# Two heads on both halves of TensorE's array in a first mixer, and its gate units in quarters

## The chip, the cores and the metric

The kernel runs on one core of a Trainium2 chip. A core has a matrix engine (TensorE, PE in the profile), two engines for elementwise work (VectorE, DVE, and ScalarE, ACT), GpSimd (POOL) and SyncE (SP, which issues most transfers). Each works through its own queue of instructions in order, and they wait for one another by semaphores. The metric is the device time of one execution in microseconds (us), lower is better.

## The reference

One block with mixture-of-experts is followed by two blocks of a second model; the change concerns the first mixer alone. For 256 tokens of width 1024:

```python
h = rmsnorm(x, g_mix[l])
proj = h @ w_in[l]
q_d, k_d, v_d, q_s, k_s, v_s, gate_d, gate_s = split_cols(proj, IN_WIDTHS)
y_dil = dilated_attention(q_d, k_d, v_d)          # 8 merged heads x 3 patterns, 64 wide
y_swa = swa_sink_attention(q_s, k_s, v_s, sinks)  # 16 heads, 64 wide, window 128
mixed = (jax.nn.sigmoid(gate_d) * (y_dil @ w_br_dil[l])
         + jax.nn.sigmoid(gate_s) * (y_swa @ w_br_swa[l]))
x = x + mixed @ w_out[l]
```

A merged head of the dilated attention takes one softmax over the scores of its three patterns together, since the weights by which the three results are added come from their own sums. All is computed in float32.

## The kernel before

Each engine's program is written out in order by hand. Weights come as units of 128 x 2048 numbers. SyncE loads a unit into one of six raw buffers, ScalarE writes its high part (`whi`, L1332), VectorE the remainder (`wlo`, L1905), and TensorE multiplies three combinations of high and low parts. There are three buffers for each part, so a unit's parts are made while the two units ahead of it are in use. `ahead(u)` issues them up to unit u + 2, and the transfer of a later unit waits for the low part.

The 32 steps of the first mixer are listed in `steps_a`: 16 for the dilated heads (three score matrices each), then 16 for the sliding window (two heads in each). A step takes 128 queries; with the first half of the queries it sees 128 keys, with the second 256. `attend` on TensorE issues, in step a:

1. a part of one of eight gate units, if it is due (`gates_between`: half a unit of 24 matmuls in every even step);
2. the scores of step a + 2 (L821), once VectorE has read all scores up to step a + 1 out of PSUM (`att_biased`);
3. the transposes of step a's probabilities (`turn`, L831), once VectorE has made them (`att_probs`) and ScalarE has copied the last ones out (`att_pt`);
4. probabilities times values for step a - 1 (`mix`, L845).

A dilated head's scores contract over 64 rows, which are the lower or the upper 64 of the array as the head is even or odd, and its mix fills the lower or the upper 64 columns.

VectorE's `attend` does in step a: the probabilities of step a (`probs`, L2090 and L2092 or L2100), the copy of a finished pair of heads (L2112), then for step a + 2 bias (L2066), maximum (L2071 or L2074) and its scaled negative (`bias_max`), and in every fourth step a unit's low part. ScalarE does the exponentials of step a + 1, the copy of step a's transposed probabilities into `PT` (`copy_turned`, L1444, two buffers), and in every fourth step a unit's high part (L1332) and the copy of a finished gate unit out of PSUM (`evac`, L1403). In step 21 the finished dilated result is split in high and low part (`ah`, `al`).

After step 31 come the branch units (`u_br`, L664 from 285.55 on), four pairs of a dilated and a sliding-window unit.

## Time and profile before

| | |
|---|---|
| time, median of 3 runs | 1794.43 us (1793.86 to 1796.72) |
| profiled execution, its own time | 1794.68 us |
| span of the profiled execution (first to last instruction) | 1792.9 us |
| PE busy | 1692.4 us (94%) |
| DVE busy | 1288.1 us (72%) |
| ACT busy | 1025.4 us (57%) |
| mean granted clock of TensorE | 0.977 |

The span is 1.8 us shorter than the profiled execution's time. Busy shares are means over stages with different limits; which engine others wait for is read from each stage. In the rows below L12 is line 12 of the kernel before; PE is matmul, PEld its weight load; a float32 matmul leaves two records. A row's second number is the time from the first record's start to the last one's end; ends of matmuls are modelled, so costs are better read from one group's start to the next group's.

### The profile page before, as it was taken

How to read it: one execution, taken by the hardware profiler on the slowest of the kernel's cores; microseconds unless marked ns; L12 is line 12 of the kernel's file. 1: busy time of each engine (PE TensorE's matmuls, PEld its weight loads, DVE VectorE, ACT ScalarE, POOL GpSimd, SP SyncE). 2: the span in 40 equal slices, each digit the busy share in tenths (PEclk: the TensorE clock that was granted, in tenths of full speed). 3: DMA queues.
4: the chain of work that ended last, by engine and by line, in shares of the span. 5: the costliest groups of instructions: out<-in, count | busy, mean ns of one | idle time of the engine just before them, and what ended most of it. 6: DMA issues, size and time to landing. Idle time of an engine off the chain costs nothing.

```text
span 1792.9 us, 29597 instructions
## 1 busy us (share of the span) xinstructions
PE 1692.4 (94%) x11478; PEld 1506.8 (84%) x11478; DVE 1288.1 (72%) x1439; ACT 1025.4 (57%) x1127; POOL 63.8 (4%) x56
## 2 busy tenths in 40 slices
PE   8999999889999999999989879799999999799998
PEld 7998878878877676777768769799998999799997
DVE  6545687675589999999988866675555888575554
ACT  4333465454588999999986354353344484343432
POOL 0000000000000000000006400000000020000000
PEclk9998999989999999999999989999999999899999
DMA  9662114065699999999997424255554465245540
GB/s 322 187 188 71 48 60 157 8 258 197 234 360 422 423 422 423 423 422 423 422 400 241 137 90 142 94 175 190 177 185 141 150 203 169 67 166 187 187 140 24
DMA packets 186768, 391.74 MB, mean 218 GB/s; under 512 B 6960, under 2 KB 152112, under 8 KB 162096
## 3 DMA queue, kind: packets, MB, share of 16 engines
q1 hardware_dynamic: 185008, 383.89, 58.7%
q0 software_dynamic: 1664, 6.52, 1.0%
q8 instruction: 66, 1.08, 0.3%
q14 instruction: 30, 0.25, 0.0%
HBM read 379.77 MB, written 10.62 MB: 218 GB/s over the span
## 4 chain that ended last, share of the span: by engine, by line
PE 63%; DMA 14%; DVE 14%; issue 5%; ACT 3%; SPq 0%; DVEq 0%; POOL 0%; ACTq 0%; POOLq 0%
DMA raw<-w_e_up_dram 12%; PE ps L664 10%; PE ps L665 10%; PE ps L669 10%; DVE wlo L1905 6%; PE ps L1004 3%; PE ps L821 3%; PE ps L892 2%; PE ps L890 2%; PE ps L959 2%; PE ps L898 2%; PE ps L953 2%; PE ps L845 2%; PE ps L955 2%; ACT whi L1332 1%
## 5 line engine op out<-in xcount | busy, mean ns | idle before, releaser
L1905 DVE TENSOR_TENSOR wlo<-raw,whi 128x2048 fp32r<-128x2048 f32 (+3 forms) x358 | 812.6, 2281 | 223.3 <-ACT whi L1332 216.2
L1332 ACT ACTIVATE whi<-raw 128x2048 fp32r<-128x2048 f32 (+3 forms) x358 | 675.4, 1890 | 339.7 <-PE ps L669 197.6
L664 PE MATMUL ps<-xh,whi 128*128 128x256 f32 x800 | 200.6, 290 | 11.7 <-DVE xl L1918 10.8
L665 PE MATMUL ps<-xl,whi 128*128 128x256 f32 x800 | 197.7, 286 | 0.0
L664 PE MATMUL ps<-xb_h,whi 128*128 128x256 f32 x768 | 188.2, 285 | 5.2 <-DVE arena L1987 5.2
L665 PE MATMUL ps<-xb_l,whi 128*128 128x256 f32 x768 | 187.5, 284 | 0.0
L664 PEld LDWEIGHTS ps<-xh,whi 128*128 128x128 f32 x800 | 155.9, 195 | 13.7 <-issue 11.6
L953 PE MATMUL ps<-whi,xh 128*128 128x512 f32 x528 | 160.3, 396 | 0.0
L665 PEld LDWEIGHTS ps<-xl,whi 128*128 128x128 f32 x800 | 155.9, 195 | 0.2
L664 PEld LDWEIGHTS ps<-xb_h,whi 128*128 128x128 f32 x768 | 148.4, 193 | 5.7 <-DVE arena L1987 5.6
L665 PEld LDWEIGHTS ps<-xb_l,whi 128*128 128x128 f32 x768 | 148.4, 193 | 0.1
L959 PE MATMUL ps<-wlo,xh 128*128 128x512 f32 x528 | 143.6, 396 | 3.1 <-DVE wlo L1905 2.9
L959 PEld LDWEIGHTS ps<-wlo,xh 128*128 128x128 f32 x528 | 97.0, 188 | 32.5 <-DVE wlo L1905 12.8
L953 PEld LDWEIGHTS ps<-whi,xh 128*128 128x128 f32 x528 | 97.4, 188 | 20.7 <-ACT whi L1332 0.4
L669 PE MATMUL ps<-xh,wlo 128*128 128x256 f32 x800 | 104.1, 283 | 0.0
L669 PE MATMUL ps<-xb_h,wlo 128*128 128x256 f32 x768 | 100.0, 283 | 0.0
L669 PEld LDWEIGHTS ps<-xh,wlo 128*128 128x128 f32 x800 | 99.6, 192 | 0.0
L669 PEld LDWEIGHTS ps<-xb_h,wlo 128*128 128x128 f32 x768 | 95.6, 192 | 0.0
L890 PE MATMUL ps<-ah,whi 128*128 128x256 f32 x352 | 85.4, 283 | 0.0
L892 PE MATMUL ps<-al,whi 128*128 128x256 f32 x352 | 85.4, 283 | 0.0
L1004 PE MATMUL ps<-whi,ah 128*64 128x512 f32 (+1 forms) x280 | 75.8, 396 | 8.6 <-ACT ah L1511 3.9
L1004 PE MATMUL ps<-wlo,ah 128*64 128x512 f32 (+1 forms) x280 | 76.4, 398 | 2.1 <-DVE wlo L1905 0.3
(429 smaller groups left out, 2896.8 us busy)
## 6 DMA issues: line engine op xcount, KB each, us to landing
raw<-w_e_gate_dram SPq DMA_DIRECT2D x64, 1024.0 KB, 10.6
raw<-w_e_up_dram SPq DMA_DIRECT2D x64, 1024.0 KB, 10.2
raw<-w_e_down_dram SPq DMA_DIRECT2D x64, 1024.0 KB, 10.5
raw<-ffn_w_gate_up_dram SPq DMA_DIRECT2D x44, 1024.0 KB, 5.1
raw<-w_in_dram SPq DMA_DIRECT2D x30, 1024.0 KB, 5.6
raw<-ffn_w_down_dram SPq DMA_DIRECT2D x22, 1024.0 KB, 4.9
raw<-xa_w_kv_dram SPq DMA_DIRECT2D x16, 1024.0 KB, 5.5
raw<-xa_w_q_dram SPq DMA_DIRECT2D x8, 1024.0 KB, 5.0
```

Of the source, the lines that this page charges most:

```text
L664: nc.tensor.matmul(o[b], wh, h, start=b == 0 and a == 0, stop=False, skip_group_check=True)
L665: nc.tensor.matmul(o[b], wh, l, start=False, stop=False, skip_group_check=True)
L669: mm = nc.tensor.matmul(o[b], wl, h, start=False, stop=b == len(blocks) - 1 and a == len(parts) - 1, skip_group_check=True)
L821: mm = nc.tensor.matmul(o, q, k, start=a == 0, stop=a == len(pairs) - 1)
L845: mm = nc.tensor.matmul(ps[lo:lo + w, 4 + y % 2, k * T + step["qt"] * P:k * T + step["qt"] * P + P], v, PT[s % 2][:, g * per + kt, :], sta ...
L890: nc.tensor.matmul(o, wh[:, k, cols], ah[:, 2 * (j % 2) + k, :], start=first and c % 2 == 0 and k == 0, stop=False, skip_group_check=True)
L892: nc.tensor.matmul(o, wh[:, k, cols], al[:, 2 * (j % 2) + k, :], start=False, stop=False, skip_group_check=True)
L953: nc.tensor.matmul(o, h[:, k, :], wh[:, k, :], start=part == 0 and k == 0, stop=False)
L959: mm = nc.tensor.matmul(ps[:, s % 2 + 2 * up, :], rows[s][0][:, k, :], wl[:, k, :], start=False, stop=part == 1 and k == 3)
L1004: mm = nc.tensor.matmul(o, src[s % 2][:, 2 * half + k, 0:w], weights[:, k, cols], start=start and k == 0, stop=stop and k == 1)
L1332: nc.scalar.activation(whi[u % HL][:, 0:n], raw[u % RAW][:, 0:n], ACT.Copy).then_inc(hi_ready, 1)
L1905: v.tensor_tensor(wlo[u % HL][:, 0:n], raw[u % RAW][:, 0:n], whi[u % HL][:, 0:n].bitcast(F32), ALU.subtract).then_inc(lo_ready, 1)
```

## The change

The dilated steps are listed in another order: for each pair of heads first both heads with 128 keys, then both with 256. TensorE issues the scores of two such steps together, one matmul of the one head after one of the other, on the lower and the upper 64 rows, into banks of their own; where both write one bank the last matmul waits for the first. The mixes of two steps are issued together likewise, on the lower and the upper 64 columns. VectorE still takes one step after the other. Probabilities get four transposed buffers in place of two. A gate unit is computed in four parts, one in every step; ScalarE makes the high part in the second of four steps and copies the finished gate unit out in the fourth (before: both in the third). The dilated result's high part is made in step 22 and its low part in step 25 (before: both in 21). No arithmetic is added or left out.

```diff
         def score_bank(step, g):
 
+            if "head" in step:
+                bank, at = 0 if step["head"] == 0 else 5, g * T
+                if step["nk"] == P:
+                    bank, at = step["head"], g * P
+                elif g == 2:
+                    bank, at = 1, step["head"] * T
+                return ps[:, bank, at:at + step["nk"]]
             at = g * T if len(step["scores"]) == 3 else g * 512
             return ps[:, at // 512, at % 512:at % 512 + step["nk"]]
+
+        def mixed_bank(step, y):
+
+            return ps[:, 4 if "head" in step else 4 + (y + step.get("flip", 0)) % 2, :]
+
+        def turned_in(PT, s, step):
+
+            return PT[s % 4 if "head" in step else s % 2]
+
+        def turned_free(s, step):
+
+            if "head" in step:
+                return s - 3
+            return s - 3 if s in (2 * DIL_HEADS, 2 * DIL_HEADS + 1) else s - 1
...
-                for hh in range(DIL_HEADS):
-                    lo = HD * (hh % 2)
-                    for qt in range(2):
+                for pair, qt, head in product(range(DIL_HEADS // 2), range(2), range(2)):
+                        hh, lo = 2 * pair + head, HD * head
...
-                                          pv=[(lo, 0, pv)], last=hh % 2 == 1 and qt == 1,
+                                          head=head, pv=[(lo, 0, pv)], last=hh % 2 == 1 and qt == 1,
...
-                                          pv=pv, last=qt == 1, y=[qs[:, c, :]]))
+                                          flip=1, pv=pv, last=qt == 1, y=[qs[:, c, :]]))
...
-        PT_first = [x[:, 3 * b:3 * b + 3, :].rearrange("p c (b q) -> p (c b) q", q=P) for b in range(2)]
+        PT_first = [v.rearrange("p c (b q) -> p (c b) q", q=P)
+                    for v in (x[:, 0:3, :], x[:, 3:6, :], sg[:, 8:11, :], sg[:, 11:14, :])]
...
+            def fourth_unit(u, part):
+
+                _, kc, n = units[u]
+                if part == 0:
+                    st["bank"] = lin_bank()
+                    weights_in(u)
+                b, ks = part // 2, range(part % 2 * kc // 2, (part % 2 + 1) * kc // 2)
+                wh, wl = wview(whi, u, kc, n), wview(wlo, u, kc, n)
+                mm = triple(st["bank"][:, b, :], [(wh[:, k, b * P:b * P + P], wl[:, k, b * P:b * P + P], xh[:, k, :],
+                                                   xl[:, k, :]) for k in ks],
+                            first=part % 2 == 0, last=part % 2 == 1)
+                if part == 3:
                     mm.then_inc(unit_used, 1)
...
+            def score_two(s, first, second):
+
+                if s >= 1:
+                    pe.wait_ge(att_biased, s)
+                turns = ((0, 2), (1, 0), (0, 0), (1, 1), (0, 1), (1, 2))
+                wide = first["nk"] > P
+                for n, (a, g) in enumerate(turns):
+                    step = (first, second)[a]
+                    q, k = step["scores"][g][0]
+                    if n == 5 and wide:
+                        pe.wait_ge(third_scored, st["third"])
+                    mm = nc.tensor.matmul(score_bank(step, g), q, k, start=True, stop=True)
+                    if n == 0 and wide:
+                        st["third"] += 1
+                        mm.then_inc(third_scored, 1)
+                mm.then_inc(att_scored, 2)
+
+            def mix_two(s, first, second, PT):
+
+                y = st["y"]
+                pe.wait_ge(att_pt, s + 2)
+                if y >= 1:
+                    pe.wait_ge(att_out, y)
+                at, per = first["qt"] * P, first["nk"] // P
+                n = len(first["pv"][0][2])
+                for a in range(n):
+                    for b, step in enumerate((first, second)):
+                        lo, _, pv = step["pv"][0]
+                        v, g, kt = pv[a]
+                        mm = nc.tensor.matmul(mixed_bank(step, y)[lo:lo + HD, at:at + P], v,
+                                              turned_in(PT, s + b, step)[:, g * per + kt, :], start=a == 0,
+                                              stop=a == n - 1)
+                        if a == n - 1:
+                            mm.then_inc(att_mixed, 1)
+                if second["last"]:
+                    st["y"] += 1
...
+                def two(a):
+                    return a < len(steps) and "head" in steps[a]
...
+                if two(0):
+                    score_two(base, steps[0], steps[1])
+                else:
+                    score(base, steps[0])
+                    score(base + 1, steps[1])
                 for a, step in enumerate(steps):
                     s = base + a
                     if between:
                         between(a)
-                    if a + 2 < len(steps):
+                    if two(a + 2):
+                        if a % 2 == 0:
+                            score_two(s + 2, steps[a + 2], steps[a + 3])
+                    elif a + 2 < len(steps):
                         score(s + 2, steps[a + 2])
                     turn(s, step)
-                    if a >= 1:
+                    if a >= 1 and two(a - 1):
+                        if a % 2 == 0:
+                            mix_two(s - 2, steps[a - 2], steps[a - 1], PT)
+                    elif a >= 1:
                         mix(s - 1, steps[a - 1], PT)
...
             def gates_between(a):
-                if a % 2 == 0:
-                    feature_unit(u_in[23 + a // 4], half=a % 4 // 2)
+                fourth_unit(u_in[23 + a // 4], a % 4)
...
             def copy_turned(s, step, PT):
                 act.wait_ge(att_turned, s + 1)
-                if s >= 2:
-                    act.wait_ge(att_mixed, s - 1)
+                if turned_free(s, step) > 0:
+                    act.wait_ge(att_mixed, turned_free(s, step))
+                to = turned_in(PT, s, step)
                 n = len(step["scores"]) * step["nk"] // P
-                last = nc.scalar.activation(PT[s % 2][:, 0:min(n, 4), :],
+                last = nc.scalar.activation(to[:, 0:min(n, 4), :],
                                             ps[:, 2, 0:min(n, 4) * P].rearrange("p (b q) -> p b q", q=P), ACT.Copy)
...
             def gates_out(a):
                 k = a // 4
-                if a == 21:
+                if a == 22:
                     split_high(qd[:, 0:4, :], ah[:])
-                if a % 4 == 2:
-                    u = u_in[23 + k]
+                u = u_in[23 + k]
+                if a % 4 == 1:
                     ahead(u)
+                if a % 4 == 3:
                     evac(u, st["lin"], sg[:, 2 * k:2 * k + 2, :])
                     st["lin"] += 1
...
-                        v.tensor_copy(y_of(st["yk"], w), ps[:, 4 + st["y"] % 2, 0:w * T].rearrange("p (c t) -> p c t",
-                                                                                    c=w)).then_inc(att_out, 1)
+                        v.tensor_copy(y_of(st["yk"], w),
+                                      mixed_bank(step, st["y"])[:, 0:w * T].rearrange("p (c t) -> p c t",
+                                                                                      c=w)).then_inc(att_out, 1)
...
                 if a == 21:
                     dve.wait_ge(att_out, 4)
                     dve.sem_inc(h_ready, 1)
+                if a == 25:
                     split_low(qd[:, 0:4, :], ah[:], al[:])
                 if a % 4 == 3:
                     ahead(u_in[23 + a // 4])
```

TensorE's order in the dilated part, before: steps 4 and 5, from behind the gate half of step 4 (left out), with scores of steps 6 and 7 (`ps<-arena`, L821), transposes of 4 and 5 (`c` holds the identity, `scr` the probabilities, L831) and mixes of 3 and 4 (`x` holds the transposed probabilities, `arena` the values, L845).

```order
L821 MATMUL ps<-arena 128x128 [waits att_biased]
L821 MATMUL ps<-arena 128x128 x2
L831 MATMUL ps<-c,scr 128x128 [waits att_pt,att_probs]
L831 MATMUL ps<-c,scr 128x128 x2
L845 MATMUL ps<-x,arena 64x128 [waits att_pt]
L845 MATMUL ps<-x,arena 64x128 x5
L821 MATMUL ps<-arena 128x256 [waits att_biased]
L821 MATMUL ps<-arena 128x256 x2
L831 MATMUL ps<-c,scr 128x128 [waits att_pt,att_probs]
L831 MATMUL ps<-c,scr 128x128 x5
L845 MATMUL ps<-x,arena 64x128 [waits att_pt]
L845 MATMUL ps<-x,arena 64x128 x2
```

The same place after the change: steps 4, 5 and the beginning of 6, each behind a gate quarter (left out). L872 are scores, L905 transposes, L890 mixes.

```order
L872 MATMUL ps<-arena 128x256 [waits att_biased]
L872 MATMUL ps<-arena 128x256 x4
L872 MATMUL ps<-arena 128x256 [waits third_scored]
L905 MATMUL ps<-c,scr 128x128 [waits att_pt,att_probs]
L905 MATMUL ps<-c,scr 128x128 x2
L890 MATMUL ps<-arena 64x128 [waits att_pt]
L890 MATMUL ps<-arena 64x128 x11
...
L905 MATMUL ps<-c,scr 128x128 [waits att_pt,att_probs]
L905 MATMUL ps<-c,scr 128x128 x2
...
L872 MATMUL ps<-arena 128x128 [waits att_biased]
L872 MATMUL ps<-arena 128x128 x5
L905 MATMUL ps<-c,scr 128x128 [waits att_pt,att_probs]
```

The scores of steps 6 and 7 stand together in step 4, with one more wait, and the mixes of steps 2 and 3 behind the transposes of step 4; step 5 has only its gate quarter and transposes. Each transpose still waits for its own step's probabilities.

ScalarE's order at the end of the mixer, before: the copies of steps 29, 30 and 31 (`x<-ps`), the exponentials of step 31 between (`sm`, `scr`), the high part of a branch unit (`whi<-raw`), the last gate unit's copy (`arena<-ps`) and the split behind the mixer (`xh`).

```order
L1444 ACTIVATE x<-ps 128x512 [waits att_mixed,att_turned]
L1426 ACTIVATE sm<-rows,sm 128x1 [waits att_max]
L1426 ACTIVATE sm<-rows,sm 128x1
L1434 ACTIVATE scr,sm<-scr,sm 128x256 x2
L1444 ACTIVATE x<-ps 128x256 [waits att_mixed,att_turned]
L1332 ACTIVATE whi<-raw 128x2048 [waits unit_used,raw_landed2]
L1403 ACTIVATE arena<-ps 128x512 [waits unit_used]
L1444 ACTIVATE x<-ps 128x512 [waits att_mixed,att_turned]
L1347 ACTIVATE xh<-arena 128x512 [waits unit_used,h_ready] x4
```

The same after the change, from the copy of step 29 on:

```order
L1533 ACTIVATE x<-ps 128x512 [waits att_mixed,att_turned]
L1420 ACTIVATE whi<-raw 128x2048 [waits unit_used,raw_landed2]
L1514 ACTIVATE sm<-rows,sm 128x1 [waits att_max]
L1514 ACTIVATE sm<-rows,sm 128x1
L1522 ACTIVATE scr,sm<-scr,sm 128x256 x2
L1533 ACTIVATE x<-ps 128x256 [waits att_mixed,att_turned]
L1533 ACTIVATE x<-ps 128x512 [waits att_mixed,att_turned]
L1491 ACTIVATE arena<-ps 128x512 [waits unit_used]
L1435 ACTIVATE xh<-arena 128x512 [waits unit_used,h_ready] x4
```

The high part moved from behind the copy of step 30 to behind that of step 29, ahead of the exponentials of step 31, and the gate unit's copy to behind the copy of step 31.

## Rows read from the trace of the kernel before

**Rows 1.** Table of stretches: us, busy time (records) by engine, PEclk, DMA, GB/s.

```profile
152.00:160.00 8.00, 6.63 (x22) 4.91 (x21) 3.40 (x10) 0.71 (x2) 0.00 (x0) 0.50 0.00 0
176.66:194.56 17.90, 17.90 (x127) 15.14 (x126) 12.20 (x31) 8.37 (x17) 0.00 (x0) 1.00 0.09 30
280.00:288.00 8.00, 6.32 (x59) 5.38 (x58) 4.87 (x11) 5.41 (x11) 1.07 (x1) 1.00 0.09 14
```

**Rows 2.** Timeline of PE, two dilated steps: start, us, line, operation, records.

```profile
176.66 0.39 PE L682 MATMUL ps<-xh,whi 128*128 128x256 f32 x1
176.88 0.28 PE L683 MATMUL ps<-xl,whi 128*128 128x256 f32 x1
...
179.73 0.93 PE L821 MATMUL ps<-arena 64*128 64x128 f32 x6
180.59 0.55 PE L831 MATMUL ps<-c,scr 128*128 128x128 f32 x3
181.06 1.52 PE L845 MATMUL ps<-x,arena 128*64 128x128 f32 x12
182.52 1.56 PE L821 MATMUL ps<-arena 64*128 64x256 f32 x6
184.01 0.87 PE L831 MATMUL ps<-c,scr 128*128 128x128 f32 x6
184.81 0.87 PE L845 MATMUL ps<-x,arena 128*64 128x128 f32 x6
185.61 0.39 PE L682 MATMUL ps<-xh,whi 128*128 128x256 f32 x1
```

**Rows 3.** Timeline of PE, sliding-window steps, scores, transposes and one mix.

```profile
232.14 0.37 PE L821 MATMUL ps<-arena 64*128 64x128 f32 x1
232.15 0.37 PE L821 MATMUL ps<-x,arena 64*128 64x128 f32 x1
...
232.56 0.44 PE L831 MATMUL ps<-c,scr 128*128 128x128 f32 x2
...
234.38 0.48 PE L821 MATMUL ps<-arena 64*128 64x256 f32 x1
...
235.02 0.66 PE L831 MATMUL ps<-c,scr 128*128 128x128 f32 x4
...
239.83 0.67 PE L845 MATMUL ps<-x,arena 128*64 128x128 f32 x8
```

**Rows 4.** Timeline of DVE, dilated steps.

```profile
199.98 0.15 DVE L2090 RECIPROCAL sm<-sm 128x1 f32<-128x1 f32 x1
...
200.70 0.42 DVE L2112 COPY arena<-ps 128x256 f32<-128x256 f32 x1
202.02 1.08 DVE L2066 SCALAR_TENSOR_TENSOR scr<-c,ps 128x256 f32<-128x256 f32 x3 [0.90 <-PE ps L821]
...
204.20 0.15 DVE L2090 RECIPROCAL sm<-sm 128x1 f32<-128x1 f32 x1
```

**Rows 5.** Timeline of DVE, sliding-window steps and a low weight part.

```profile
239.58 0.48 DVE L2066 SCALAR_TENSOR_TENSOR scr<-c,ps 128x128 f32<-128x128 f32 x2 [1.76 <-PE ps L821]
...
242.08 0.74 DVE L2066 SCALAR_TENSOR_TENSOR scr<-c,ps 128x256 f32<-128x256 f32 x2
...
243.85 2.29 DVE L1905 TENSOR_TENSOR wlo<-raw,whi 128x2048 fp32r<-128x2048 f32 x1
246.06 0.15 DVE L2089 TENSOR_TENSOR sm<-sm 128x2 f32<-128x2 f32 x1
...
246.85 0.48 DVE L2066 SCALAR_TENSOR_TENSOR scr<-c,ps 128x128 f32<-128x128 f32 x2
```

**Rows 6.** Timeline of PE, the mixer's first scores and its end.

```profile
152.99 1.65 PE L821 MATMUL ps<-arena 64*128 64x128 f32 x6 [0.59 <-DVE x L2388]
...
284.95 0.67 PE L845 MATMUL ps<-x,arena 128*64 128x128 f32 x8 [1.68 <-ACT x L1444]
285.55 0.39 PE L664 MATMUL ps<-ah,whi 128*128 128x256 f32 x1
```

More of the change, by code:

```diff
@@ L14 @@
 from contextlib import ExitStack
+from itertools import product
 import numpy as np
@@ L263, in build @@
                                                                sem("att_exp"), sem("att_probs"))
+        third_scored = sem("third_scored")
         att_turned, att_pt, att_mixed, att_out = sem("att_turned"), sem("att_pt"), sem("att_mixed"), sem("att_out")
@@ L643, in _ @@
         def _(pe):
-            st = dict(lin=0, sq=0, step=0, xl=0, y=0, fresh=False)
+            st = dict(lin=0, sq=0, step=0, xl=0, y=0, fresh=False, third=0)
             def high_in(u, i=None, step=6):
@@ L717, in feature_unit @@
                 if half == 1:
+                    mm.then_inc(unit_used, 1)
+            def fourth_unit(u, part):
[9 more added lines that the diff above has]
+                if part == 3:
                     mm.then_inc(unit_used, 1)
@@ L844, in mix @@
                         w = v.shape[1]
-                        mm = nc.tensor.matmul(ps[lo:lo + w, 4 + y % 2, k * T + step["qt"] * P:k * T + step["qt"] * P + P],
-                                              v, PT[s % 2][:, g * per + kt, :], start=a == 0, stop=a == len(pv) - 1)
+                        at = k * T + step["qt"] * P
+                        mm = nc.tensor.matmul(mixed_bank(step, y)[lo:lo + w, at:at + P], v,
+                                              turned_in(PT, s, step)[:, g * per + kt, :], start=a == 0,
+                                              stop=a == len(pv) - 1)
                 mm.then_inc(att_mixed, 1)
@@ L852, in attend @@
                 base = st["step"]
-                score(base, steps[0])
-                score(base + 1, steps[1])
+                def two(a):
[5 more added lines that the diff above has]
+                    score(base + 1, steps[1])
                 for a, step in enumerate(steps):
@@ L1440, in copy_turned @@
                 act.wait_ge(att_turned, s + 1)
-                if s >= 2:
-                    act.wait_ge(att_mixed, s - 1)
+                if turned_free(s, step) > 0:
+                    act.wait_ge(att_mixed, turned_free(s, step))
+                to = turned_in(PT, s, step)
                 n = len(step["scores"]) * step["nk"] // P
-                last = nc.scalar.activation(PT[s % 2][:, 0:min(n, 4), :],
+                last = nc.scalar.activation(to[:, 0:min(n, 4), :],
                                             ps[:, 2, 0:min(n, 4) * P].rearrange("p (b q) -> p b q", q=P), ACT.Copy)
                 if n > 4:
-                    last = nc.scalar.activation(PT[s % 2][:, 4:n, :],
+                    last = nc.scalar.activation(to[:, 4:n, :],
                                                 ps[:, 3, 0:(n - 4) * P].rearrange("p (b q) -> p b q", q=P), ACT.Copy)
```

## The prediction

> **Words.** The first mixer runs 32 steps: 0 to 15 dilated, 16 to 31 sliding-window. A step with 128 keys is narrow, one with 256 wide. Per step TensorE does scores, turn (transposing the probabilities) and mix (probabilities times values), and between them work on the gate units; VectorE does "bias and maximum" (scores out of PSUM, maximum, its negative) and "probabilities" (reciprocal, scaling). Costs are from one group's start to the next one's.
>
> **What bounds the kernel now.** I read the table by stretches first. While the dilated steps run, TensorE is busy 17.90 of 17.90 us and VectorE 12.20, which takes in one low weight part [rows 1]. So here, and not in the kernel at large, TensorE's own queue is the limit. The timeline of TensorE shows what fills a narrow and a wide step, from one gate half to the next (176.66 to 185.61, 8.95 us): gate half 3.07, narrow scores 0.86, three transposes 0.47, wide mix 1.46, wide scores 1.49, six transposes 0.80, narrow mix 0.80 [rows 2]. Nothing waits. Each head uses 64 of 128 rows of the array in its scores and 64 of 128 columns in its mix.
>
> The sliding-window steps already issue two heads together, and there the two halves do work at one time: score records of the two heads start 0.01 apart [rows 3]. Two heads' narrow scores take 0.42 (232.14 to 232.56) and wide ones 0.64 (234.38 to 235.02); eight mix records of two heads span 0.67, where six of one head in a dilated step span 0.87 [rows 2, 3].
>
> After step 16 VectorE and TensorE hand over to one another, and 284.95 is the last wait: TensorE stood 1.68 us for ScalarE's copy of step 31's turned probabilities; the first branch unit begins at 285.55 [rows 6]. From there on TensorE's work is the same, so I take the shift of this point as the shift of the end.
>
> **The change, part by part.**
>
> *Dilated scores and mixes in pairs.* Per four steps (two heads, narrow and wide) TensorE now spends twice 8.95, that is 17.90. Three score matmuls per head, alternating between heads, should cost what one head's cost now: 0.86 for the two narrow heads and 1.49 for the two wide ones. The bounds are half of one-head time (this value) and three times what one pair costs in a sliding-window step, 1.26 and 1.92; both include a hand-over that a longer stream pays once, so I take the former. For the mixes likewise 0.80 and 1.46. Saved: 0.86 + 1.49 + 0.80 + 1.46 = 4.61.
>
> *Gate units in quarters.* A quarter is half of 3.07 plus one more slow first matmul: 0.22 from the first to the second (176.66 to 176.88), where the rest go at 0.12 [rows 2], so 1.54 + 0.10 = 1.63. Four of them are 6.52 against 6.14: +0.38. Four steps then cost 17.90 - 4.61 + 0.38 = **13.67**. Whether the others keep up I check along one such stretch, from gate part 0: wide scores end at 3.12, turns are at 3.12, 6.68, 9.64 and 12.87, narrow scores end at 9.64. VectorE: wide bias and maximum 2.18 (202.02 to 204.20), wide probabilities 0.72 (199.98 to 200.70), copy of a finished pair at most 0.42 [rows 4], narrow probabilities at most 0.72. From 3.22 it does bias and maximum (5.40), probabilities (6.1, wanted at 6.68), copy (6.5), bias and maximum (8.7), probabilities (9.4, wanted at 9.64). That is the tightest place, 0.2 of slack. The wait added (the wide score of the second head's third group waits for the first head's) is on a matmul five places earlier in the queue: nothing. VectorE's whole work, 12.2, is below 13.67.
>
> *Opening.* The first scores start at 152.99, at the low level: the granted clock is 0.50 over 152 to 160, 1.2 GHz [rows 1, 6]. At twice the costs above: two narrow scores to 154.7, a quarter to 157.5, wide scores to 160.3; then turn 0, quarter, turn 1, quarter, narrow scores, turn, mix, quarter, turn at the high level or partly so. Step 4's gate part then starts at 169.5 to 170.5, by whether the clock comes back before 160 (TensorE no longer pauses after the first scores) or after; I take 170.0. Before it is 176.66 [rows 2]: -6.7.
>
> *Steps 4 to 15.* Three stretches of 13.67 end at 211.0; step 17's scores in the last one delay its end to 211.2. But turn 16 needs probabilities 16, which VectorE makes after a low weight part. Counted from gate part 12, the third quarter ends at 8.78, scores 16 take 0.42, turn, mix and quarter run to 12.43, scores 17 are in at 13.2; then bias and maximum 1.77 (242.08 to 243.85), low part 2.21 (to 246.06), probabilities 0.79 (to 246.85) [rows 5]: turn 16 at 170.0 + 27.3 + 18.0 = 215.3. Before it is 232.56 [rows 3]: **-17.2**.
>
> *Steps 16 to 31.* Here only the gate parts, the high weight part and the splitting of the dilated result move. TensorE's four steps are 6.52 + 2 x (0.42 + 0.37 + 0.60 + 0.64 + 0.58 + 0.44) = 12.6, where 0.37 (232.56 to 232.93) is the narrow turn [rows 3] and 0.58, 0.44 and 0.60 are parts and twice that by the number of records. VectorE's are 12.3: narrow bias and maximum, wide probabilities and copy together 2.50 (239.58 to 242.08), wide bias and maximum 1.77, narrow probabilities 0.79, all twice, plus 2.21 [rows 5]. Neither is the limit: their chain is. From a narrow turn that waited for a low part, TensorE runs 9.55 without a pause to the wide scores three steps on (three quarters, three scores, three turns, three mixes), then VectorE needs 1.77 + 2.21 + 0.79, and hand-overs 0.2: 14.5. With halves all sixteen steps and their end take 52.99 (285.55 - 232.56) [rows 3, 6], so quarters give nothing here. Turn 16 to 20 is 15.4 (the last wide dilated mix for two heads, +0.86), 20 to 24 is 14.5, 24 to 28 14.3 (a low part of half the size, -1.1, but the split of the dilated result now stands in step 25 and holds turn 26 up by 0.9). From turn 28 to the branch unit TensorE's own work is 10.1 (three quarters, one score, four turns, five mixes), and I put down 0.75 for step 31's waits for probabilities and copy: 10.85. Sum 55.05, so the branch unit begins at 215.3 + 55.05 = 270.35. Against 52.99 that is **+2.1**. In it the end gains: the high weight part now stands in step 29, so that the copy of step 31 is no longer behind it, and the 1.68 wait shrinks to some 0.3; two more quarters after turn 28 take that back.
>
> **Sum.** -17.2 + 2.1 = **-15.1**. The profiled execution took 1794.68 (span 1792.9), 0.25 over the median of 1794.43. 1794.68 - 15.1 = 1779.6; nearer the median, **1779.4**.
>
> **A rule against the mixes.** Of the eight mix records of two heads the trace shows 0.67 where one head's rate would give 0.87 plus two more [rows 2, 3]: two column halves do overlap. The Trainium skill ("TensorE: Matmul & The Clock Gate", section Part 3: Packing small matmuls) says that a weight load overlaps matmuls in flight only when its row group differs. Two mixes share all rows, so by this rule their weight loads would stand in line; the trace disagrees in the sliding-window steps. By it the sum would be that of the third rival below.
>
> **Rivals.**
> 1. *Forecast*: halves overlap in full and TensorE stays the limit, 1779.4 (1776 to 1782). Chance 0.62, with 0.05 in it for a clock that returns earlier and a gentler chain after step 16.
> 2. *Scores overlap only as pairs do now*: 1.26 and 1.92 per four steps, +0.83 each over some 3.6 such stretches, +3: 1782.4. For it: the pairs in rows 3 are too short to show a stream. Chance 0.16.
> 3. *Mixes don't overlap* when heads alternate: +2.26 x 3.6 = +8, 1787.5. Against it: 0.67 for eight records. Chance 0.04.
> 4. *VectorE's chain becomes the limit* in the dilated steps: scores now come for two steps at once and VectorE takes them one by one, with 0.2 of slack. At 1 to 1.5 us more per four steps, +4 to +5: 1784. For it: VectorE works 12.2 of 13.67. Chance 0.12.
> 5. *It doesn't do what it says*: heads stay one after the other. Then the four steps cost 18.28, so +16.6 on the forecast: 1796, within 0.2% of before. Against it: 0.01 between two heads' starts. Chance 0.03.
> 6. *The other side: the clock.* After step 16 TensorE stands some 2 us in each four steps while VectorE makes the low part and the probabilities behind it. If the clock falls there to 0.50 and stays, a pair of steps costs twice 6.3 instead of some 7, up to +5 x 8 = 40: 1819. It decides from about four of the eight pairs at the low level. Against it: over 280 to 288, which has the wait of 1.68, the clock held 1.00 [rows 1, 6], and quarters spread TensorE's work. Chance 0.03.
>
> Less than 0.2% (3.6 us) can't be told from no change. Faster: 1, 2, 3, 4 = 0.94; same: 0.03; slower: 0.03. Range: 1776 (early clock, no loss after step 16) to 1785 (takes in 2 and most of 4), which leaves out some 0.17.
>
> **What would show it.** Right: four dilated steps in 13.7 us with TensorE without waits; six score slots of 0.11 (narrow) and 0.22 (wide) for two heads; turn 16 at about 215 and the first branch unit at about 270; VectorE's wait for wide scores about 1 us per four steps. Wrong: score slots of 0.2 and 0.3 (rival 2); waits of TensorE for probabilities before turns 2, 6, 10 (rival 4); a granted clock of 0.50 after 170 (rival 6); or, against my last term, less than 53 us from turn 16 to the branch unit, because the chain there is shorter than I added up.

## The result and the profile after

The changed kernel took 1778.84 us (median of 4 runs, 1774.78 to 1781.32) beside 1795.37 (1793.86 to 1796.72) for the kernel before: ratio 0.9906, 95% interval 0.9885 to 0.9927. The forecast of 1779.4 was right. The profiled execution took 1778.12, its span is 1776.3 (before 1792.9), and PE is busy 1677.1 us, 15.3 less than before.

The first branch unit now begins 115.74 us after the first scores (267.50 - 151.76). Before it was 132.56 [rows 6]. That is -16.8, and the span shrank by 16.6. By stretches, with the prediction's own figures between:

| from, to | before | predicted | after |
|---|---|---|---|
| first scores, gate part of step 4 | 23.67 | 17.0 | 15.12 |
| gate part of step 4, turn 16 | 55.90 | 45.3 | 44.31 |
| turn 16, turn 20 | 14.42 | 15.4 | 15.33 |
| turn 20, turn 24 | 14.53 | 14.5 | 15.93 |
| turn 24, turn 28 | 13.47 | 14.3 | 14.36 |
| turn 28, first branch unit | 10.56 | 10.85 | 10.70 |

The timeline of PE over four dilated steps answers to [rows 2]. L705 is the first matmul of a gate quarter (the other eleven are left out), L872 scores, L905 transposes, L890 mixes.

```profile
171.91 0.39 PE L705 MATMUL ps<-xh,whi 128*128 128x256 f32 x1
...
173.43 0.49 PE L905 MATMUL ps<-c,scr 128*128 128x128 f32 x3
173.68 0.36 PE L705 MATMUL ps<-xh,whi 128*128 128x256 f32 x1
...
175.28 0.94 PE L872 MATMUL ps<-arena 64*128 64x128 f32 x12
176.21 0.88 PE L905 MATMUL ps<-c,scr 128*128 128x128 f32 x6
177.01 0.88 PE L890 MATMUL ps<-x,arena 128*64 128x128 f32 x12
177.82 0.38 PE L705 MATMUL ps<-xh,whi 128*128 128x256 f32 x1
...
179.35 0.82 PE L905 MATMUL ps<-c,scr 128*128 128x128 f32 x6
179.92 0.36 PE L705 MATMUL ps<-xh,whi 128*128 128x256 f32 x1
...
181.51 1.57 PE L872 MATMUL ps<-arena 64*128 64x256 f32 x12
183.01 0.55 PE L905 MATMUL ps<-c,scr 128*128 128x128 f32 x3
183.49 1.53 PE L890 MATMUL ps<-arena 128*64 128x128 f32 x24
184.95 0.39 PE L705 MATMUL ps<-xh,whi 128*128 128x256 f32 x1
```

Twelve score records of two heads take 0.93 (175.28 to 176.21) and 1.50 (181.51 to 183.01), where one head's six took 0.86 and 1.49 [rows 2]; the mixes take 0.81 and 1.46, as one head's did. No row of TensorE shows a wait. Four steps take 13.04 in place of 17.90.

The table of stretches, first those four steps, then turn 16 to 20, 20 to 24, 24 to 28 and to the branch unit:

```profile
171.91:184.95 13.04, 13.04 (x128) 11.52 (x127) 12.01 (x31) 8.10 (x16) 0.00 (x0) 1.00 0.14 42
...
211.18:226.51 15.33, 13.36 (x116) 10.49 (x116) 12.00 (x40) 9.34 (x30) 0.00 (x0) 1.00 0.20 70
226.51:242.44 15.93, 13.95 (x100) 10.84 (x100) 12.04 (x40) 10.29 (x31) 0.00 (x0) 0.89 0.11 34
242.44:256.80 14.36, 12.55 (x100) 9.62 (x100) 11.88 (x41) 8.71 (x30) 0.00 (x0) 1.00 0.22 73
256.80:267.50 10.70, 10.14 (x85) 7.67 (x85) 7.69 (x25) 6.74 (x18) 0.00 (x0) 1.00 0.16 51
```

In the dilated steps TensorE is busy all the time, and VectorE 12.01 of 13.04. From turn 16 on neither is full, and in the second of these four the granted clock is 0.89. The timeline of PE at the places that answer to [rows 3, 6]:

```profile
151.76 1.35 PE L872 MATMUL ps<-arena 64*128 64x128 f32 x12 [0.59 <-DVE x L2479]
...
166.88 0.36 PE L705 MATMUL ps<-xh,whi 128*128 128x256 f32 x1
...
211.19 0.44 PE L905 MATMUL ps<-c,scr 128*128 128x128 f32 x2 [2.31 <-DVE scr L2190]
...
226.51 0.44 PE L905 MATMUL ps<-c,scr 128*128 128x128 f32 x2 [1.98 <-DVE scr L2190]
226.88 0.85 PE L920 MATMUL ps<-x,arena 128*64 128x128 f32 x8
227.67 0.58 PE L705 MATMUL ps<-xh,whi 128*128 128x256 f32 x1
...
230.53 0.52 PE L858 MATMUL ps<-arena 64*128 64x256 f32 x1
...
266.90 0.66 PE L920 MATMUL ps<-x,arena 128*64 128x128 f32 x8 [0.32 <-ACT x L1533]
267.50 0.38 PE L687 MATMUL ps<-ah,whi 128*128 128x256 f32 x1
```

Turns 16 and 20 (and 24, for 1.98) wait about 2 us for VectorE. Behind turn 20 the gate quarter takes 2.86 (227.67 to 230.53), where the others take 1.5 to 1.6, and the mix 0.79 in place of 0.59: TensorE is at its low level there, which makes some 1.5 of that stretch's 15.93. The wait of 1.68 at the mixer's end [rows 6] is 0.32.

What turn 20 waits for stands in VectorE's timeline (to compare with [rows 5]): the low weight part comes between the wide scores' bias and the narrow probabilities.

```profile
221.60 0.75 DVE L2156 SCALAR_TENSOR_TENSOR scr<-c,ps 128x256 f32<-128x256 f32 x2 [0.51 <-PE ps L858]
...
223.38 2.29 DVE L1995 TENSOR_TENSOR wlo<-raw,whi 128x2048 fp32r<-128x2048 f32 x1
225.59 0.15 DVE L2179 TENSOR_TENSOR sm<-sm 128x2 f32<-128x2 f32 x1
...
225.98 0.48 DVE L2190 TENSOR_SCALAR scr<-scr,sm 128x128 f32<-128x128 f32 x2
```

### The profile page after: what moved, and what is told of

It reads as the page before. It is cut to its first block, busy times and chain, and to the rows that moved or that the text cites. A ratio compares the mean times of both kernels' runs of the same rounds, so it can differ in the third digit from the quotient of the medians.

```text
span 1776.3 us, 29597 instructions
## 1 busy us (share of the span) xinstructions
PE 1677.1 (94%) x11478; PEld 1495.4 (84%) x11478; DVE 1287.6 (72%) x1439; ACT 1024.7 (58%) x1127; POOL 65.3 (4%) x56
## 3 DMA queue, kind: packets, MB, share of 16 engines
q0 software_dynamic: 1664, 6.52, 1.0%
## 4 chain that ended last, share of the span: by engine, by line
PE 63%; DVE 14%; DMA 13%; issue 6%; ACT 4%; SPq 0%; DVEq 0%; POOL 0%; ACTq 0%; POOLq 0%
PE ps L687 10%; PE ps L688 10%; PE ps L692 10%; DMA raw<-w_e_up_dram 9%; DVE wlo L1995 7%; PE ps L1093 4%; PE ps L1042 3%; PE ps L1048 3%; PE ps L979 2%; PE ps L981 2%; PE ps L987 2%; DMA raw<-w_e_down_dram 2%; PE ps L858 2%; ACT whi L1420 2%; PE ps L1044 2%
## 5 line engine op out<-in xcount | busy, mean ns | idle before, releaser
L687 PE MATMUL ps<-xh,whi 128*128 128x256 f32 x800 | 202.7, 292 | 11.9 <-DVE xl L2008 10.8
L1048 PEld LDWEIGHTS ps<-wlo,xh 128*128 128x128 f32 x528 | 97.0, 188 | 32.4 <-DVE wlo L1995 12.8
## 6 DMA issues: line engine op xcount, KB each, us to landing
raw<-w_e_gate_dram SPq DMA_DIRECT2D x64, 1024.0 KB, 10.7
```

The lines of the kernel that those rows point to most:

```text
L687: nc.tensor.matmul(o[b], wh, h, start=b == 0 and a == 0, stop=False, skip_group_check=True)
L1048: mm = nc.tensor.matmul(ps[:, s % 2 + 2 * up, :], rows[s][0][:, k, :], wl[:, k, :], start=False, stop=part == 1 and k == 3)
```

## The experiments

From the first branch unit to the end of the span the profiled executions took between 1504 and 1513 us, whatever was edited ahead of it; TensorE was busy 1421 us there in the shortest (granted clock 0.98) and 1433 in the longest (0.97), for the same number of records. So the times below carry several us that have nothing to do with the mixer, and each reading rests on the stretches of one profiled execution, worked out from the starts of turns and scores; time and ratio to the kernel before stand beside. "To 16" is from the first scores to turn 16, "four" four dilated steps (turn 8 to 12), "last" from turn 28 to the first branch unit, "all" from the first scores to there.

| kernel | to 16 | four | 16 to 20 | 20 to 24 | 24 to 28 | last | all | time, ratio [95%] |
|---|---|---|---|---|---|---|---|---|
| before | 79.57 | 17.91 | 14.42 | 14.53 | 13.47 | 10.56 | 132.56 | |
| changed | 59.42 | 13.04 | 15.33 | 15.93 | 14.36 | 10.70 | 115.74 | 1778.84, 0.9906 |
| changed, again | 58.53 | 13.05 | 16.89 | 15.99 | 14.37 | 10.70 | 116.48 | 1777.82, 0.9902 [0.9881, 0.9923] |
| pairs_only | 66.77 | 14.76 | 14.42 | 14.55 | 13.46 | 10.56 | 119.76 | 1781.68, 0.9926 [0.9903, 0.9949] |
| quarters_only | 82.94 | 19.42 | 15.33 | 15.96 | 14.35 | 10.69 | 139.26 | 1804.53, 1.0053 [1.0034, 1.0071] |
| scores_blocks | 63.29 | 13.86 | 16.75 | 15.93 | 15.87 | 10.69 | 122.53 | 1782.45, 0.9925 [0.9902, 0.9947] |
| mixes_blocks | 62.71 | 14.20 | 16.25 | 15.87 | 15.87 | 10.68 | 121.39 | 1781.22, 0.9928 [0.9907, 0.9950] |
| halves_late | 59.46 | 13.05 | 14.42 | 14.12 | 13.45 | 9.90 | 111.35 | 1774.31, 0.9894 [0.9867, 0.9921] |
| high_late | 60.03 | 13.04 | 14.42 | 14.13 | 13.45 | 10.07 | 112.10 | 1780.16 (one run) |
| low_split | 58.32 | 13.05 | 13.52 | 12.85 | 13.38 | 10.92 | 108.99 | 1774.90, 0.9892 [0.9869, 0.9915] |
| low_split_2 | 58.58 | 13.04 | 13.51 | 12.85 | 13.39 | 10.91 | 109.25 | 1770.72, 0.9869 [0.9849, 0.9889] |
| low_split_halves | 60.61 | 13.05 | 13.76 | 13.71 | 13.72 | 10.23 | 112.03 | 1774.58, 0.9886 [0.9866, 0.9906] |
| low_whole_later | 57.24 | 13.04 | 13.56 | 13.76 | 16.32 | 10.84 | 111.72 | 1774.29, 0.9889 [0.9865, 0.9912] |
| low_later | 56.32 | 13.05 | 13.52 | 12.66 | 13.78 | 10.43 | 106.70 | 1770.85, 0.9862 [0.9841, 0.9883] |

**Two heads without quarters (pairs_only).** The high part, the gate unit's copy and the split of the dilated result go back with the halves.

```diff
-                fourth_unit(u_in[23 + a // 4], a % 4)
+                if a % 2 == 0:
+                    feature_unit(u_in[23 + a // 4], half=a % 4 // 2)
```

> The changed kernel with the gate units in halves at even steps, as before; two heads still go together. My theory: the quarters are what covers VectorE. Without a quarter between turn a and turn a+1 only a mix (0.8 or 1.5 us) stands there, while VectorE needs bias and maximum and probabilities (some 2.3 narrow, 2.9 wide), so TensorE waits about 1.0 at every odd turn: four dilated steps take 15.3 to 15.5 in place of 13.04, some +8.5 in all, and the sliding-window part goes back to about 53, -3. Time about 1784 to 1785. Rival, the terms simply add as in the prediction (two heads -4.61, quarters +0.38 on their own): four dilated steps 13.3, no waits, time about 1777.

Four dilated steps take 14.76, nearer to my theory than to the rival, with smaller waits than I worked out; from turn 16 on it is the kernel before to 0.02. PE's timeline at two odd turns, a wide and a narrow one:

```profile
184.06 0.88 PE L905 MATMUL ps<-c,scr 128*128 128x128 f32 x6 [0.68 <-DVE scr L2182]
...
192.25 0.55 PE L905 MATMUL ps<-c,scr 128*128 128x128 f32 x3 [1.01 <-DVE scr L2182]
```

These two waits, 1.69 in four steps, are the whole difference to 13.04 (14.76 - 1.69 = 13.07). In the dilated steps the halves cost TensorE no more work than quarters do; what they lack is work between turn a and turn a + 1, while VectorE makes the probabilities of the second head.

**Quarters without two heads (quarters_only).** The kernel before with `fourth_unit`, the early high part, and the later copy and split.

> The kernel before with the gate units in quarters and the early high part, one head after the other as before. My theory: quarters gain nothing by themselves; four dilated steps 18.2 to 18.3 (17.90 before), +1.4 in sixteen steps, and the sliding-window steps lose 2 to 3: 1798 to 1800. Rival: a part of the gain comes from the quarters or the early high part, 1790 or less.

Alone the quarters are a loss, and a larger one than I expected: four steps take 19.42, not 18.2 to 18.3, and the time is 1804.5, not 1798 to 1800. The work came out as expected, 18.34; the rest is a wait that I had not put down, at the narrow turn behind a low part (PE's timeline):

```profile
177.81 0.55 PE L845 MATMUL ps<-c,scr 128*128 128x128 f32 x3 [1.08 <-DVE scr L2106]
```

At turn 16 the two parts alone give +3.4 and -12.8, and together -20.1, which is 10.7 more than their sum. But the openings in these figures differ in their clock (in pairs_only a wait of 2.47 at turn 1 was followed by 0.50 over 162.0 to 165.4). From turn 4 to turn 16, where the clock is 1.00 in all four kernels, the parts give +4.8 and -8.4, and together -10.8: 7.2 more than their sum. From turn 16 on quarters_only takes 56.33, the changed kernel 56.32, the kernel before and pairs_only 52.99: the whole loss there comes with the quarters and what was moved with them (halves_late below tells the two apart).

**Heads in blocks.** First the scores, then the mixes, in the order first head, second head.

```diff
-                turns = ((0, 2), (1, 0), (0, 0), (1, 1), (0, 1), (1, 2))
+                turns = ((0, 2), (0, 0), (0, 1), (1, 0), (1, 1), (1, 2))
```

> The changed kernel with the six score matmuls of two heads in another order: the three of the first head, then the three of the second. My theory: the two row halves work at one time only where neighbours in the queue belong to different heads, so two heads cost what two cost before: narrow 1.7 in place of 0.93, wide 3.0 in place of 1.50, four dilated steps 15.3 in place of 13.04, time about 1787. Rival: the order does not matter, since a waiting matmul of the second head can start beside the first head's anyway: 13.0 and 1779.

```diff
-                for a in range(n):
-                    for b, step in enumerate((first, second)):
+                for b, step in enumerate((first, second)):
+                    for a in range(n):
```

> The changed kernel with the mix matmuls of two heads in another order: all of the first head, then all of the second. My theory: column halves overlap only between neighbours of different heads, so a narrow mix takes 1.6 in place of 0.81 and a wide one 2.9 in place of 1.46, four dilated steps 15.3 in place of 13.04, time about 1787. Rival: the mixes gain from something other than the alternation, such as one hand-over and one wait for two heads, and keep most of it: 13.0 to 13.5, 1779 to 1781.

Neither theory had the size. Blocks cost 0.82 and 1.16 in four steps, a third and a half of what I put on them: wide scores take 2.03 in place of 1.50, where two heads one by one would be 2.98; wide mixes 2.38 in place of 1.46 (184.90 to 187.28), against 2.92. The table of stretches of scores_blocks, for L872 alone (PE, then PEld), shows why:

```profile
185.06:185.59 0.53, 0.53 (x2) 0.48 (x3) 1.00 0.00 0
185.59:186.35 0.76, 0.76 (x8) 0.73 (x7) 1.00 0.00 0
186.35:187.09 0.74, 0.74 (x6) 0.37 (x2) 1.00 0.46 84
```

Counted are the records that run in a stretch. One head's start some 0.22 apart, so in the middle 0.76 three or four would; seven do, beside one that began before. If records began in the order of the queue, all six of the first head's would come first, the last of them not before 186.16, and nine could not have begun by 186.35. So the second head runs beside the first before the first is through, though it stands behind it in the queue. The first stretch, 0.53, is the first head's alone, and it is what the blocks lose (2.03 - 1.50). In mixes_blocks, for L890, eight records run in the first 0.92 (184.90 to 185.82) and nine in the next 0.38, and 0.92 is again what the blocks lose. The alternation saves this time, because it lets the two halves start together.

**Halves from step 16 on (halves_late), and the high part's place (high_late).**

```diff
-                fourth_unit(u_in[23 + a // 4], a % 4)
+                if a < 16:
+                    fourth_unit(u_in[23 + a // 4], a % 4)
+                elif a % 2 == 0:
+                    fourth_unit(u_in[23 + a // 4], a % 4)
+                    fourth_unit(u_in[23 + a // 4], a % 4 + 1)
```

> The changed kernel with quarters in the dilated steps and both quarters of a half together at the even steps from step 16 on. My theory: the sliding-window steps got slower because three quarters (4.9) instead of one half (3.1) stand between a turn that waited for a low part and the wide scores that the next low part is queued behind: turn 16 to the branch unit goes from 56.3 back to 53 to 54 and the clock holds, time about 1775.5. Rival: the loss comes from VectorE's order alone, whatever TensorE does between: 56, time 1778.8.

Turn 16 to the branch unit takes 51.89 (56.32 with quarters), the clock holds 1.00 in all of it, and no wait is longer than 0.9. My theory holds, and by 1.1 more than expected. TensorE is busy 45.7 us of it, in the changed kernel 50.0, some 1.5 of that the low clock: quarters are also more work there, not only a longer chain.

```diff
-                if a % 4 == 1:
+                if a % 4 == (1 if a < 16 else 2):
                     ahead(u)
```

> The run with halves from step 16 on, with ScalarE's high weight part back in the third step of four from step 16 on. My theory (the end term of the prediction): the copy of step 31's turned probabilities is again behind the high part, the last mix waits 1.7 in place of 0.3, and the first branch unit comes 1.1 to 1.4 later: 112.5 to 112.8 after the first scores in place of 111.35. Rival: that wait has another cause and stays at 0.3: 111.4.

The wait came back, and the time did not. PE's row and, below it, ScalarE's:

```profile
264.37 0.66 PE L920 MATMUL ps<-x,arena 128*64 128x128 f32 x8 [1.19 <-ACT x L1537]
```

```profile
261.65 0.39 ACT L1537 ACTIVATE x<-ps 128x256 f32<-128x256 f32 x1 [0.78 <-PE ps L905]
261.93 1.90 ACT L1424 ACTIVATE whi<-raw 128x2048 fp32r<-128x2048 f32 x1
263.73 0.59 ACT L1537 ACTIVATE x<-ps 128x512 f32<-128x512 f32 x1
```

The copy of step 31 is again behind the high part, and the last mix waits 1.19. But in halves_late the high part stands ahead of the exponentials of step 31, and turn 31 waits 0.65, which it does not here. "Last" is 10.07 and 9.90: the move gains 0.17. Of the 0.75 in "all" the rest lies ahead of turn 16, and most of what the time is longer lies behind the branch unit (1513.3 for 1507.7). I had expected 1.1 to 1.4 for the move.

**The low part in two pieces (low_split).** From step 12 on VectorE's low part is cut into two of 1024 columns, in steps 1 and 3 of a group, each ahead of the wait for wide scores; the high part comes a step earlier.

```diff
                         out(a - 2)
+                    if early:
+                        early(a)
                     if a + 2 < len(steps):
                         bias_max(base + a + 2, steps[a + 2])
...
+            def gates_early(a):
+                if a >= 12 and a % 2 == 1 and st["lo"] < min(u_in[23 + a // 4] + HL, st["top"]):
+                    lo(st["lo"], part=a % 4 // 2)
+                    st["lo"] += a % 4 // 2
```

> The changed kernel with the low weight part, from step 12 on, in two pieces of 1024 columns, each ahead of VectorE's wait for a wide step's scores (steps of a group 1 and 3), and the high part one step earlier. My theory: VectorE stands 0.3 to 1.8 us before each wide step's scores, so a piece of 1.1 is hidden there, TensorE no longer waits some 2 us at the turns 16, 20 and 24, the clock holds, and turn 16 to the branch unit takes about 52 in place of 56.3, with turn 16 some 2 earlier: time 1773 to 1775. Rival: VectorE's chain is as long wherever the low part stands in it, 1778 to 1780.

Turn 16 to the branch unit takes 50.67, and the low clock level is gone. The table of stretches, from turn 16 on:

```profile
209.99:223.51 13.52, 13.36 (x116) 10.49 (x116) 12.05 (x41) 9.55 (x32) 0.00 (x0) 1.00 0.16 53
223.51:236.36 12.85, 12.46 (x100) 9.60 (x100) 11.80 (x40) 10.19 (x33) 0.00 (x0) 1.00 0.13 38
236.36:249.74 13.38, 12.48 (x102) 9.62 (x100) 12.03 (x41) 8.76 (x33) 0.00 (x0) 1.00 0.26 90
249.74:260.66 10.92, 9.93 (x87) 7.66 (x85) 8.42 (x26) 7.21 (x21) 0.00 (x0) 1.00 0.01 3
```

TensorE is busy 48.2 of these 50.67 and waits the rest. Turn 16 came only 1.1 earlier, not 2, since turn 14 now waits 1.41.

**Pieces in other steps, and with halves (low_split_2, low_split_halves).** In the first the pieces of steps 13 and 15 stand in steps 12 and 14 (and the high part of step 12 in step 11); the second adds the edit of halves_late.

> The low weight part in two pieces as in the run of that name, except that the pieces of steps 12 to 15 stand ahead of the scores of steps 14 and 16 (in steps 12 and 14), where VectorE waits for two heads' scores. There turn 14 waited 1.4. My theory: turn 14 no longer waits and turn 16 comes 1 to 1.5 earlier, so the first branch unit stands at 107.5 to 108 after the first scores in place of 108.99, time 1772 to 1774. Rival: VectorE has too little idle time in steps 12 to 15 (0.5 in four steps), the wait only moves to another turn: 109 and 1775.

The rival was right: turn 13 waits 0.80 and turn 14 0.81 in place of 1.41 at turn 14, and "all" is 109.25. That its time was 4 us lower than low_split's comes from behind the mixer: its profiled execution took 1506.3 there, low_split's 1512.5.

> The same with the quarters of a half together at the even steps from step 16 on. My theory: with the low pieces hidden TensorE's own work is the limit (50.7 from turn 16 to the branch unit against 50.4 of work), so fewer hand-overs save at most 0.8 and waits of VectorE's chain at odd turns take more back: 51 to 53, time 1773 to 1776. Rival: halves gain as they did with the low part whole (-4.4): 47 to 48, 1769 to 1771.

51.4 from turn 16 on, as expected, but for other terms than mine. The 50.4 of work in the expectation was no measurement: TensorE is busy 48.2 with quarters (low_split_2) and 45.9 with halves. So halves save 2.4 of work where I allowed 0.8, and add 3.1 of waits (0.76 at each of five turns among them). With the low part whole they paid (halves_late), with its pieces hidden they don't.

**The pieces a group later, whole or cut (low_later, low_whole_later).** Three buffers hold low parts, so none has to be made in steps 12 to 15.

```diff
+                if a >= 16 and (a % 2 == 1 or a == 30) and st["lo"] < min(u_in[23 + a // 4] + HL - 1, st["top"]):
+                    lo(st["lo"], part=(a + 1) % 4 // 2 ^ 1)
```

> The changed kernel with VectorE's low weight part in two pieces as in low_split, but a group of four steps later: none in steps 12 to 15, then pieces ahead of the scores' wait in steps 17, 19, 21, 23 and on. Three buffers hold the low parts, so it is still in time. My theory: turn 14 (1.41 of wait in low_split) and turn 16 (2.31 in the changed kernel) wait for nothing, and from turn 16 on TensorE's own work stays the limit: first branch unit 107.0 to 107.8 after the first scores, in place of 115.74 in the changed kernel, time 1769 to 1772. Rival: the low parts pushed together at the end (one more is left for step 31) bring a new wait behind the last mix: 109 to 110, 1772 to 1775.

> As low_later, with each low part whole (2.29) ahead of the scores' wait in steps 17, 21, 25 and 29. It tells the place from the cutting. My theory: the place does most of it, but the idle time there is 1.2 for a pair of steps, so a whole part delays the wide scores by about 1 and a turn behind them by 0.5 to 1 per group: 2 to 4 longer than low_later from turn 16 on, 1773 to 1775. Rival: only the place counts, and it is as fast as low_later.

> The changed kernel once more, beside low_later on the same chip, for the ratio and for the clock. My theory: each wait of about 2 us at turns 16, 20 and 24 can be followed by a stretch of the low clock level of some 1.5 us in price, and in which of them it happens differs from run to run: turns 20 to 24 and 24 to 28 take 14.4 or 15.9 each, the first branch unit stands 114 to 117.5 after the first scores, time 1775 to 1781. Rival: the fall belongs to a place in the program and is the same in each run: 15.93, 14.36 and 115.7.

Turn 16 now waits for nothing, and from there it takes 50.39, of which TensorE is busy 48.2; turn 26 still waits 1.30. VectorE's timeline in low_later:

```profile
210.67 1.22 DVE L1996 TENSOR_TENSOR wlo<-raw,whi 128x1024 fp32r<-128x1024 f32 x1
212.42 0.75 DVE L2159 SCALAR_TENSOR_TENSOR scr<-c,ps 128x256 f32<-128x256 f32 x2 [0.53 <-PE ps L858]
...
217.91 1.22 DVE L1996 TENSOR_TENSOR wlo<-raw,whi 128x1024 fp32r<-128x1024 f32 x1
219.04 0.74 DVE L2159 SCALAR_TENSOR_TENSOR scr<-c,ps 128x256 f32<-128x256 f32 x2
```

Behind the first piece VectorE still waits 0.53 for the scores; behind the second they are there. A whole part in the same place costs 4.1 more (54.48), just above the 2 to 4 that I expected, and brings back a wait and the low level (PE's timeline):

```profile
244.87 0.69 PE L905 MATMUL ps<-c,scr 128*128 128x128 f32 x2 [2.37 <-DVE scr L2193]
```

low_later reaches the branch unit first of all kernels run. Its time is 1770.85 (1769.86 to 1771.81) beside 1777.82 for the changed kernel and 1795.76 for the one before, on the same chip; by time it can't be told from low_split_2 (1770.72). It is 9.0 ahead of the changed kernel at the branch unit, 0.9 of that in an opening that had the clock at 1.00 by chance (so it was in the changed kernel's second profile). That second profile bears out my theory of the clock in part: the low level also followed turn 16 there (16.89 in place of 15.33), but behind turn 20 it stood in both, and behind turn 24 in neither.

## Why the prediction was right

**Halves in pairs.** Right to 0.1: 0.93 and 1.50 for the scores, 0.81 and 1.46 for the mixes. Rivals 2, 3 and 5 fall with these rows. For rival 3 the Trainium skill ("TensorE: Matmul & The Clock Gate", Part 3: Packing small matmuls) had a weight load overlap matmuls in flight only where the row group differs; 24 mix records with equal row groups in 1.46 us, as long as one head's 12 took, say otherwise here. The section also lets loads into a background weight buffer go ahead, so what fails here is the "only".

**Four dilated steps.** 13.67 was too high by 0.63, and the mis-sized term is the quarters with the turns between them. I put 6.52 for four quarters, and they took 6.24: a whole slow first matmul went on each, though half of 3.07 already holds half of one. And I kept the turns at 0.47 and 0.80; a turn that goes over into a gate quarter takes 0.25 and 0.57, which makes 0.44 in four steps. The Trainium skill ("TensorEngine Tiling (Array Packing)", Key Properties) says that a change of tiling mode drains TensorE. The trace fits it, though no row shows a drain as such: gate matmuls and transposes both use 128*128, and a quarter's last matmul goes over into transposes in 0.12 (173.31 to 173.43), but into scores, on 64*128, in 0.21 (175.07 to 175.28).

**The quarters' worth.** The step that was wrong in kind: I costed quarters as +0.38 of work and gave no thought to what two heads without them would wait for. pairs_only shows that they save 1.69 of waiting in four steps, because a quarter stands ahead of each turn. The sum did not suffer, since it was made for both together, and rival 4 (VectorE's chain as the limit) stayed away for that reason: some 0.5 of wait for wide scores is left to VectorE in four steps, not the 1 that I named. In steps 4 to 15 only turn 14 waited for it (0.43).

**Opening.** 17.0 forecast, 15.12 measured: the clock rose at about 155.5 rather than near 160. It was allowed for in the range, and it is in part luck. Up to turn 2 the program is the same in low_later and low_split_halves, yet the first had the clock at 1.00 and the second at 0.79 (table of stretches of each, from the first scores to turn 2):

```profile
151.90:162.39 10.49, 8.86 (x78) 7.61 (x78) 8.77 (x26) 5.23 (x10) 0.00 (x0) 1.00 0.00 0
...
153.01:165.13 12.12, 11.01 (x78) 9.57 (x78) 8.77 (x26) 5.24 (x10) 0.00 (x0) 0.79 0.00 0
```

To the gate part of step 4 the same program took 14.2 to 15.8, the changed kernel's second profile 14.20. All are below 17.0. The kernel before has one profile alone, so how much of its 23.67 was chance isn't shown.

**Steps 16 to 31.** Three of the four stretches came within 0.15. The other is 15.93 for 14.5, and the low clock level is the 1.4: rival 6 in small. It named the place and the cause rightly and the price wrongly; the full level was back within 3.5 us each time, so it costs 1.5 and not 40. What I held against it, that the clock had stood through a wait of 1.68, was one sample (see the last section). That quarters lengthen this part (+3.3, some 1.5 of it the clock) and halves do not is shown by pairs_only, quarters_only and halves_late. In halves_late and low_split no wait there is over 0.9 and the clock holds 1.00; that it holds because the waits are short is likely, but not shown, since it also held behind turn 16 (2.31) in the changed kernel's first profile.

**The end.** The wait of 1.68 shrank to 0.32 as forecast, but the high part's place is worth only 0.17 (high_late, with halves from step 16 on; with quarters it wasn't run): the other end of the same queue lost what the copy won.

**Sum.** Up to turn 16 it was 2.9 too cautious (-20.1 for -17.2), behind it 1.2 too kind (+3.3 for +2.1). The two errors offset in part, and that the forecast came within 0.6 us of the measured time owes something to this. For the profiled execution the sum gave 1779.6, and it took 1778.12: -16.6 for -15.1. What stands ahead of the mixer (1.2 less than in the profile before) and behind it (1.4 more) nearly cancelled.

## What to carry to other kernels

An edit that seems to cost work can be what makes another pay: when two pieces of work are joined, look for what filled the time between their consumers, and put something there. Long work on an in-order engine (here a 2.3 us weight part) belongs ahead of that engine's own wait, in pieces no longer than the wait, not between its input's arrival and the result that others stand for. And a wait that is removed from an end is worth only what the next chain leaves: read "last" as a whole stretch, not the wait alone.

## What was unexpected of the hardware

Score matmuls of the second head started beside those of the first while the first head still had some in the queue: seven records began in 0.76 us where one head's three or four would (scores_blocks). The Trainium skill ("TensorE: Matmul & The Clock Gate", Part 3: Packing small matmuls) has matmuls start and end strictly in program order; for two-record float32 matmuls on different halves the starts of the records here do not agree.

After waits of 1.7 to 2.5 us the clock fell to 0.50 in some places and not in others, and after turn 24 (wait 1.98 in the changed kernel) only in the two runs with blocks. Behind the wait of 1.68 at the mixer's end it held in the kernel before [rows 1, 6], and behind the 1.69 there in pairs_only it was 0.50 over 271.2 to 274.6. Behind shorter waits between turn 1 and the first branch unit, up to 1.41, it held 1.00 in every profile. What decides it is left open. The 1504 to 1513 us behind the first branch unit go with the clock as well, and why it differs from run to run is open too.
